# One core, fp32 layer step: the weights' sums of six block products made in the attention stage, the seven products in another order, the gated features' sums one stage later

## The reference, cut to what matters

```
xn = rms_norm(x, norm_mix_w)
rq, rk, rv, rg, cq, ckv, kpe, ga, gb = split_columns(xn @ w_in)
...
ret_y, mla_y, new_state = mixer_core(rq, rk, rv, q, ckv, kpe, w_ukv)
ret_branch = (head_group_norm(ret_y, ret_gn_w).astype(x.dtype) * jax.nn.silu(rg)) @ w_ret_o
mla_branch = mla_y @ w_mla_o
merged = jax.nn.sigmoid(ga) * ret_branch + jax.nn.sigmoid(gb) * mla_branch
h = x + merged @ w_out
g, u = jnp.split(rms_norm(h, norm_ffn_w) @ w_gate_up, 2, axis=-1)
h = h + (jax.nn.silu(g) * u) @ w_down
```

## Time and profile before

| | us |
|---|---|
| median of 3 runs | 2095.4 (2094.5 to 2097.5) |
| the profiled execution | 2096.48 |
| its span in the profile | 2094.6 |
| PE busy in it | 2002.0 (96%) |
| DVE busy | 1319.5 (63%) |
| ACT busy | 796.8 (38%) |
| POOL busy | 632.2 (30%) |

### The profile page before, as it was taken

One profiled execution on the slowest core, in us unless ns is written; L12 is line 12 of the kernel. 1 busy time (PEld: TensorE's weight loads), 2 busy tenths in 40 slices (PEclk: granted clock), 3 DMA queues, 4 the chain that ended last, 5 costly groups with the idle time before them and its releaser, 6 DMA issues.

```text
span 2094.6 us, 35179 instructions
## 1 busy us (share of the span) xinstructions
PE 2002.0 (96%) x14160; PEld 1933.2 (92%) x14160; DVE 1319.5 (63%) x2002; ACT 796.8 (38%) x1390; POOL 632.2 (30%) x488
## 2 busy tenths in 40 slices
PE   8989999999999989799999989999999999999997
PEld 8978888889988989699999979999999999999997
DVE  6567776765555558977867896655555555432257
ACT  5334444442332245365554325534444444310010
POOL 0110000001343445725223663544444444200000
PEclk9999999999999999899999989899999999999999
DMA  8301010151444466654755533122323232663412
GB/s 308 110 24 32 24 32 25 34 216 45 139 164 163 165 247 206 233 192 150 256 208 181 189 120 133 57 99 93 116 88 121 84 125 84 246 256 113 173 54 86
DMA packets 114241, 282.37 MB, mean 135 GB/s; under 512 B 13344, under 2 KB 30688, under 8 KB 106528
## 3 DMA queue, kind: packets, MB, share of 16 engines
q1 hardware_dynamic: 114080, 280.12, 38.2%
HBM read 191.85 MB, written 88.23 MB: 134 GB/s over the span
## 4 chain that ended last, share of the span: by engine, by line
PE 79%; DVE 12%; issue 3%; ACT 2%; DMA 2%; POOL 1%; SPq 0%; DVEq 0%; ACTq 0%; POOLq 0%
PE ps L1148 24%; PE ps L1149 23%; PE ps L1150 23%; DVE s_lo L2133 1%; PE ps L1249 1%; PE ps L1341 1%; PE ps L1243 1%; DVE t_lo L2133 1%; DVE tmp L2140 1%; DVE hg L2498 1%; DVE hg L2490 1%; DVE negmax L2362 1%; DVE hg L2502 1%; DMA xn_lo<-xn_spill 1%; PE ps L1404 1%
## 5 line engine op out<-in xcount | busy, mean ns | idle before, releaser
L1148 PE MATMUL ps<-s_hi,t_hi 128*128 128x272 f32 x1344 | 395.8, 295 | 30.8 <-DVE s_lo L2133 30.8
L1149 PE MATMUL ps<-s_hi,t_lo 128*128 128x272 f32 x1344 | 393.9, 293 | 0.0
L1150 PE MATMUL ps<-s_lo,t_hi 128*128 128x272 f32 x1344 | 392.7, 292 | 0.0
L1148 PE MATMUL ps<-sx_hi,t_hi 128*128 128x272 f32 x1232 | 357.1, 290 | 0.0
L1149 PE MATMUL ps<-sx_hi,t_lo 128*128 128x272 f32 x1232 | 356.9, 290 | 0.0
L1148 PEld LDWEIGHTS ps<-s_hi,t_hi 128*128 128x128 f32 x1344 | 260.0, 193 | 33.7 <-DVE s_lo L2133 24.4
L1149 PEld LDWEIGHTS ps<-s_hi,t_lo 128*128 128x128 f32 x1344 | 259.6, 193 | 0.0
L1150 PEld LDWEIGHTS ps<-s_lo,t_hi 128*128 128x128 f32 x1344 | 259.5, 193 | 0.0
L1150 PE MATMUL ps<-sx_lo,t_hi 128*128 128x272 f32 x880 | 255.3, 290 | 0.0
L1148 PEld LDWEIGHTS ps<-sx_hi,t_hi 128*128 128x128 f32 x1232 | 234.8, 191 | 0.3 <-DVE t_lo L2133 0.2
L1149 PEld LDWEIGHTS ps<-sx_hi,t_lo 128*128 128x128 f32 x1232 | 234.3, 190 | 0.0
(11 more groups left out here) (283 smaller groups left out, 5114.8 us busy)
## 6 DMA issues: line engine op xcount, KB each, us to landing
t_row<-in_weights SPq DMA_DIRECT2D x48, 512.0 KB, 5.7
y_spill<-hg_r SPq DMA_DIRECT2D x44, 544.0 KB, 3.4
yd<-y_spill SPq DMA_DIRECT2D x22, 1088.0 KB, 5.6
s_raw<-s_x SPq DMA_DIRECT2D x21, 1088.0 KB, 5.8
w_stage<-in_weights SPq DMA_DIRECT2D x35, 512.0 KB, 3.9
raw<-in_weights SPq DMA_DIRECT2D x22, 512.0 KB, 5.2
hg<-in_weights SPq DMA_DIRECT2D x22, 512.0 KB, 5.3
d_stage<-in_weights SPq DMA_DIRECT2D x24, 384.0 KB, 3.0
```

Of the source, the lines that this page charges most:

```text
L1148: nc.tensor.matmul(out, wh, xh, start=start, stop=False, skip_group_check=onto)
L1149: nc.tensor.matmul(out, wl, xh, start=False, stop=False, skip_group_check=onto)
L1150: return nc.tensor.matmul(out, wh, xl, start=False, stop=stop, skip_group_check=onto)
```

## The change

The change has five parts.

1. **Jobs.** The weights' sums T of all six octets are made during attention, in 48 jobs. A job is one half (two of four 128-columns) of the four weights' blocks of one octet and one p: SP loads 2 x 256 KB into `job_tile[job % 2]`, POOL does four operations of 128x256, each on the result of the one before (`job_sums`), and SP stores 512 KB to `t_sums` in device memory. `job_slots` puts them at six T steps of each head (four in the last): `job_store(job - 1)`, then `job_load(job)`. The second tile is where `x_inv` was, which is stored and loaded again. While the jobs run, weights' items 9 to I_RET + 3 use a single stage (the load of item n waits for the low part of item n - 1). The rotary sum of heads 1 to 7 goes from POOL to DVE.
2. **Octets' rows.** POOL makes no T sums in the octets. Each step's row is loaded: three from the weights, four from `t_sums`, 84 loads of half rows in pairs over three `t_rows` buffers, each of which waits for the low part three steps before.
3. **Order of the seven products.** C11 is ready after step 1, C12 after 4, C22 after 5, C21 after 6 (before: C21 after 3, C11 after 4, C22 after 5, C12 after 6). ACT makes 4 copies an octet instead of 12, and DVE 24 reads of banks instead of 16; in MIX_OUT the first product is added to three results by 12 more DVE operations.
4. **Gated features' sums.** POOL's 16 operations on the gated features are done in GATE_A's units 4 to 19 instead of in GATE_RET's last units and GATE_A's first, and SP stores them at units 14 and 22.
5. **MIX_OUT and pair 0.** The merged features are no longer stored to `s_m` and loaded again, but are taken from SBUF; of the squares for the feed-forward norm 12 are made in MIX_OUT and 4 in pair 0; pair 0 takes its products in the order 0, 1, 3, 2, 5, 4, 6, with its fourth sums on DVE and its third on POOL.

```diff
-FIRST_ORDER = (0, 3, 2, 1, 4, 5, 6)
+FIRST_ORDER = (0, 1, 3, 2, 5, 4, 6)
...
-ROW_OF_STEP = (0, 0, 4, 4, 2, 1, 3)
-OPENING_STEPS = (0, 4, 5)
...
+OPENING_STEPS = (0, 2, 5)
+ROWS = 3
...
+SUM_PLACE = {2: 0, 6: 1, 3: 2, 5: 3}
+JOBS = OCTETS * 4 * 2
...
+RESULT_STEP = (1, 4, 5, 6)
+RESULT_OF = {1: C11, 4: C12, 5: C22, 6: C21}
...
+def job_slots():
+    steps = [(h, at) for h in range(MH) for at in ((0, 1, 3, 4, 6, 7) if h + 1 < MH else (0, 1, 3, 5))]
+    return {step: 2 + i for i, step in enumerate(steps)}
...
+FIRST_JOB_ITEM, LAST_JOB_ITEM = 9, I_RET + 3
...
+def stage_of(n):
+    return 0 if FIRST_JOB_ITEM <= n <= LAST_JOB_ITEM else n % 2
...
+        x_inv_spill = nc.dram_tensor("x_inv_spill", (P, TOK), F32, kind="Internal").ap()
+        t_sums = nc.dram_tensor("t_sums", (OCTETS, 4, P, 4, 4 * P), F32, kind="Internal").ap()
...
-                    sp.wait_ge(w_low, n - 1)
+                    sp.wait_ge(w_low, n if FIRST_JOB_ITEM <= n <= LAST_JOB_ITEM else n - 1)
...
-                if g == 0 and what == "M" and kind in "KR":
+                if what == "M" and (kind, g) == ("K", 0):
                     items(mla_item(h, kind) + 2, mla_item(h, kind) + 3)
+                if what == "M" and (kind, g) == ("V", NG - 1) and h % 2 == 0:
+                    items(mla_item(h, "R") + 2, mla_item(h, "R") + 3)
...
+            def job_store(job):
+                sp.wait_ge(job_sum, 4 * job + 4)
+                o, p, half = job // 8, job // 2 % 4, job % 2
+                sp.dma_start(t_sums[o, p, :, :, 2 * P * half:2 * P * (half + 1)], job_tile[job % 2][:, :, :])\
+                  .then_inc(job_out[job % 2], 16)
...
+            def job_load(job):
+                if job == 0:
+                    sp.wait_ge(w_low, FIRST_JOB_ITEM - 1)
+                elif job == 1:
+                    sp.wait_ge(spill_out, 16 * (2 * KT + 1))
+                else:
+                    sp.wait_ge(job_out[job % 2], 16 * (job // 2))
+                o, p, half = job // 8, job // 2 % 4, job % 2
+                first, step = OCTET_ITEMS[o]
+                first += step * p
+                for tile in range(2):
+                    sp.dma_start(job_tile[job % 2][:, 2 * tile:2 * tile + 2, :].rearrange("p h (k c) -> p h k c", c=P),
+                                 W[first + 4 * step * tile].rearrange("p (h k) c -> p h k c", h=2)
+                                 [:, :, 2 * half:2 * half + 2, :]).then_inc(job_in[job % 2], 16)
...
+                    if s[0] == "T":
+                        if (h, transposed) in slots:
+                            job = slots[h, transposed]
+                            job_store(job - 1)
+                            job_load(job)
+                        transposed += 1
...
-            def row_load(o, r, half):
+            def row_load(j, half):
...
+                if j >= ROWS:
+                    sp.wait_ge(ot_low, 4 * (j - ROWS) + 2 * half + 2)
...
+                if s in SUM_PLACE:
+                    src = t_sums[o, 2 * half:2 * half + 2, :, SUM_PLACE[s], :].rearrange("n p c -> p n c")
...
+                    if p in (0, 2) and j + ROWS < STEPS * OCTETS:
+                        row_load(j + ROWS, p // 2)
...
-            def quadrant_copy(o, c, p):
-                u = UNITS * o + 4 * (C11, C12, C22).index(c) + p
...
+            def first_product_copy(o, p):
+                u = UNITS * o + p
...
+                    if h:
+                        dve.wait_ge(p_free, own[u] + 1)
+                        dve.wait_ge(rot_low, r)
+                        nc.vector.tensor_tensor(rot_total[:, 0:c1 - c0], rot_cos[:, 0:c1 - c0], rot_sin[:, 0:c1 - c0],
+                                                ALU.add).then_inc(rot_sum, 1)
...
-            def result_read(o, c, p):
-                u = UNITS * o + 12 + 4 * c + p
...
+            def bank_read(o, s, p):
+                dve.wait_ge(oct_done, UNITS * o + 4 * s + p + 1)
                 bank = ps[:, 2 * p:2 * p + 2, 0:QUARTER]
+                c = {1: C11, 2: C21, 3: C22, 4: C12, 5: C22, 6: C21}[s]
+                if o == MIX_OUT:
+                    at = quarters(piece(o, c, p)[:, :])
+                    if s == 1:
+                        wait_piece(dve, o, c, p)
+                    nc.vector.tensor_tensor(at, bank, at, ALU.add).then_inc(o_read, 1)
...
+            def first_product_added(p):
+                dve.wait_ge(oct_done, UNITS * MIX_OUT + p + 1)
+                for c in (C12, C22, C21):
+                    wait_piece(dve, MIX_OUT, c, p)
+                    at = quarters(piece(MIX_OUT, c, p)[:, :])
+                    ins = nc.vector.tensor_tensor(at, ps[:, 2 * p:2 * p + 2, 0:QUARTER], at, ALU.add)
...
+            def job_sums(job):
+                b11, b21, b12, b22 = [job_tile[job % 2][:, i, :] for i in range(4)]
+                pool.wait_ge(job_in[job % 2], 32 * (job // 2 + 1))
+                nc.gpsimd.tensor_tensor(b22, b22, b12, ALU.subtract).then_inc(job_sum, 1)
+                pool.wait_ge(job_sum, 4 * job + 1)
+                nc.gpsimd.tensor_tensor(b12, b12, b11, ALU.subtract).then_inc(job_sum, 1)
+                pool.wait_ge(job_sum, 4 * job + 2)
+                nc.gpsimd.tensor_tensor(b11, b22, b11, ALU.add).then_inc(job_sum, 1)
+                pool.wait_ge(job_sum, 4 * job + 3)
+                nc.gpsimd.tensor_tensor(b21, b21, b11, ALU.subtract).then_inc(job_sum, 1)
...
-            def octet_sums(o, name, p):
-                b11, b12, b21, b22, t3 = [t_rows[r][:, p, :] for r in range(5)]
-                if name == "T3":
...
-                    nc.gpsimd.tensor_tensor(t3, b22, b12, ALU.subtract).then_inc(ot_sum, 1)
...
+            def gated_sums(name, p):
+                if name == "S1":
+                    wait_final(pool, GATE_RET, C21, p)
+                    nc.gpsimd.tensor_tensor(bm(C21, p), bm(C21, p), bm(C22, p), ALU.add).then_inc(m_sum, 1)
+                elif name == "S2":
...
+                    if o == GATE_A and 4 <= n < 20:
+                        gated_sums(("S1", "S2", "S3", "S4")[n % 4], n // 4 - 1)
```

More of the change, by code:

```diff
@@ new lines, in octet_transfers, with result_store @@
+                late, m = divmod(g - 5, UNITS)
+                if late == GATE_RET and m // 4 in (1, 4, 5) and m % 2:
+                    operand_store({1: 0, 4: 1, 5: 6}[m // 4], m % 4 // 2)
+                if o == GATE_A and n in (14, 22):
+                    for s in (2, 3, 4, 5):
+                        operand_store(s, n // 16)
+            def result_store(o, c, half):
+                tile, (c0, c1) = tile_of(c, 2 * half), tail_of(c)
+                sp.wait_ge(c_act, 16 * o + 4 * c + 2 * half + 2)
+                sp.dma_start(gate_spill[o - GATE_A, tile:tile + 2, :, c0:c1].rearrange("n p c -> p n c"),
+                             acc_tiles(c, slice(2 * half, 2 * half + 2))).then_inc(c_out[c], 16)
@@ L2067, in _ @@
                     act.wait_ge(y_done, 2 * pair)
[L2068 removed]
+                    part(u3, pair, "X")
                 if pair == 0:
@@ new lines, in bank_read @@
+                if s < 4 and o == GATE_A:
+                    wait_final(dve, GATE_RET, c, p)
+                elif s < 4 and o == GATE_B or (o, s) == (BRANCH_MLA, 1):
+                    dve.wait_ge(c_out[c], 32 if o == GATE_B else 64)
+                elif s in (2, 3) and o == BRANCH_RET:
+                    dve.wait_ge(c_out[c], 64)
+                elif s in (2, 3) and o == BRANCH_MLA:
+                    dve.wait_ge(m_gated, 4 * (c - 1) + p + 1)
+                if s > 1:
+                    kept = acc(C12, p) if s < 5 else acc(c, p)
+                    nc.vector.tensor_tensor(quarters(acc(c, p)), bank, quarters(kept), ALU.add).then_inc(o_read, 1)
+                elif o in (GATE_RET, GATE_A, GATE_B):
+                    if o == GATE_RET and p == 0:
+                        dve.wait_ge(consts_in, 64)
+                    nc.vector.tensor_tensor(quarters(acc(c, p)), bank, quarters(x_inv[:, 0:HALF]), ALU.mult)\
+                      .then_inc(o_read, 1)
+                else:
+                    wait_piece(dve, o, c, p)
+                    if o == BRANCH_RET and p == 0:
+                        for step in range(STEPS):
+                            dve.wait_ge(sm_out[step], SY_OUT)
+                    dst = bm(c, p) if o == BRANCH_RET else acc(c, p)
+                    nc.vector.tensor_tensor(quarters(dst), bank, quarters(piece(o, c, p)[:, :]), ALU.mult).then_inc(o_read, 1)
@@ L2573, in gated_low @@
+            for tiles in (slice(0, 2), slice(2, 4)):
+                operand_low(2, S2_AT - 2 + tiles.stop // 2, acc_tiles(C11, tiles), tiles)
+            for p in range(4):
+                fourth_sum(p)
             def gated_low(pair, half):
```

818 lines of the change are left out of this document (371 added, 447 removed).

## The result

| | us |
|---|---|
| kernel before, median of 4 runs | 2095.3 |
| changed kernel, median of 4 runs | 2138.1 (2137.0 to 2139.2) |
| ratio, with its 95% interval | 1.0201 (1.0188 to 1.0213) |
| span of its profile | 2135.3 |

The change makes the kernel slower by 2%, 42.8 us. The forecast was slower by 10.6 us with a range that ended at 2134, 4 us short. The profile's spans give the split: the first octet's first product starts at 839.1 us instead of 765.9, which is 73.2 us lost, and from there to the end it takes 1296.2 us instead of 1328.7, which is 32.5 won.

The account below looks back on a forecast made before the run. PE was taken to bound the kernel, its stalls being what can be won. From the profiled 2096.5 us, -31 for the octets and +42 for attention gave 2107.5, or 2106 against the median; range 2068 to 2134.

Parts of the forecast that it names:

- the octets' sum: GATE_RET to pair 0: PE's stalls and clock losses shrink, -31 us in sum, between -18 and -40.
- attention's term: Attention: the jobs' serial cycle delays the `xn_lo` loads and with them the kernel, +42 us.
- C: Attention: time of one job's cycle, L plus POOL's sums plus wakes; taken as 8.4 us, bounds 7.3 and 9.7.
- the hole beside `xn_hi`: End of attention: 5.6 us added to 41 cycles, about 4 for standing behind the jobs' and `xn_hi`'s bytes.
- behind `xn_lo`: After the `xn_lo` loads, up to the octets: no further delay was added.
- Rival 2: Octets: they bring 10 us instead of 31, the stall moving to DVE's added bank reads; 2127 us, chance 0.11.
- L: Job cycle: time from the store's issue to the second load's landing, taken as 5.1 us, bounds 4.0 and 6.3.
- rival 3: Attention: DVE slows POOL's four sums, adding 1.4 us to C, 58 us; above 2150; chance 0.06 with others.
- every microsecond of theirs is one of the kernel's: End of attention: PE already waits for the `xn_lo` loads, so their delay adds in full to the kernel's time.
- Rival 1: Attention: the jobs keep pace, C at 7.3 to 7.75, time some 2067 to 2079 us; chance 0.23.
- The prediction's own sign of being wrong: C at 7.6 or less, PE waiting more for DVE's negmax or `p_exp`, or stalls in GATE_B.
- The page's estimate: Job cycle: 2.0 us a transfer plus bytes at 436 GB/s gives L 4.4, C 7.7, total near 2077 us.

Follow-up runs that it names:

- run 4: Kernel before, with POOL's T sums in the octets cut to one column except four in GATE_RET: 2077.1 us, ratio 0.9916.
- run 5: Changed kernel without the 48 jobs, plus 30 POOL operations on idle scratch in GATE_RET and GATE_A: 2079.6 us, 12.7 more than without them.
- Run 9: Changed kernel in its own store-then-load order, with jobs seven to a head in heads 0 to 5 and four in head 6: 2156.6 us, ratio 1.0291.
- Run 10: The fastest version with the four POOL operations of each job cut to one column, all transfers kept: 2066.4 us.
- the fastest version: Changed kernel with each job's loads ahead of the previous job's store, seven jobs a head and four in head 6: 2077.5 us, ratio 0.9916.

## Why the prediction was wrong

The mechanism, the sign and the octets' sum were right; the size of attention's term was not: forecast +42, measured +73.2, and this error of 31 us put the time outside the range. By place it is 16.7 us from C, 5.3 from the hole beside `xn_hi`, 11.2 behind `xn_lo`, and 1.8 less at the start.

**The octets**, forecast -31: measured -32.5. By place: GATE_RET and GATE_A -5.8 and -16.7 (forecast -21 together), BRANCH_MLA and MIX_OUT -9.0 and +0.6 (forecast -8), pair 0 -1.2 (forecast -2), the rest of the feed-forward stages nothing. The stall in BRANCH_MLA went wholly, and what I left as stalls is all in MIX_OUT. That POOL beside DVE makes this stall was shown from both sides, by runs 4 and 5. Run 4 gives 20 of the 32 us to the T sums alone; most of GATE_RET's and BRANCH_MLA's came only with the order and the later gated sums. Rival 2, which left 21 us of the stall in place, is out.

**The cycle**, forecast C = 8.4 as L 5.1 + 0.1 + 3.2 + 0.05. (These make 8.45; taking 8.4 left out 2 us over 41 cycles.) Measured over the 40 cycles from the store of job 1 (137.90 us) to that of job 41 (490.64): 8.82 on average, which is 5.35 + 0.07 + 3.37 + 0.03. The row taken for L, a pair of 1088 KB, was near: in thirty of the forty cycles L is 5.0 to 5.4, 5.15 on average. In the other ten it is 5.56 to 6.95, and these lift its mean to 5.35. What they share is open: three of them have nothing on SP between the loads and the next store. And where DVE works beside POOL, a sum takes up to 1.2 us instead of 0.74 (the one at 146.77 us takes 1.22, with DVE's `w_lo` at 146.69 to 147.38). That is rival 3 in small, 0.17 us to a cycle instead of 1.4. Together 0.42 us times 40, 16.7 us: the step that failed is "I take 8.4", taken from one row where a mean over disturbed ones was needed, times 41.

**The hole beside `xn_hi`**: the 5.6 us that I added to 41 even cycles, 4 of them for standing behind bytes, are 7.8 in the 41st cycle (16.2 us) and 3.1 behind it. With these 5.3 us more, 16.7 from the mean of C and 1.8 less at the start, `xn_lo` came at 510.0 instead of the forecast 489.7.

**Behind `xn_lo`**: forecast nothing. Measured 11.2 us: the delay is 62.0 us at the issue of `xn_lo` and 73.2 at the octets' start. This second step failed too: "every microsecond of theirs is one of the kernel's" ended the sum at `xn_lo`. The late rows themselves add nothing: PE goes on behind them at 527.04 instead of 468.75, 58.3 us late (the last of them takes 11.6 us in the chain instead of 14.4). But the jobs 43 to 47 are not done, and their sums stand in POOL's program too, ahead of the retention's rotary sums (L2803). POOL, DVE and PE there:

```profile
551.08 0.99 POOL L2803 TENSOR_TENSOR rq<-tmp,tmp 128x384 f32<-128x384 f32 x1
552.18 0.56 DVE L2201 TENSOR_TENSOR tmp<-ps,cos 128x384 f32<-128x384 f32 x1 [13.44 <-POOL rq L2803]
553.97 0.55 PE L1203 MATMUL ps<-pt_hi,v_hi 128*128 128x256 f32 x1 [10.48 <-issue]
```

DVE had the products for L2803 ready at 534.9 us. POOL first summed two more jobs, waiting for their loads each time, and came to L2803 at 551.08. DVE stood for 13.4 us, and PE for 10.5, until DVE had read the bank at 553.9. The profile names nothing for PE's wait; in the program PE's unit there waits for the bank read of the unit before it, which is DVE's. The other 4.4 of the 14.9 us between 58.3 and 73.2 are open. Run 9, which has all jobs ahead of `xn_lo`, has no such wait and loses 2.4 us there instead of 11.2.

**Hidden under it**: DVE's contention with the jobs, which I put at some 3 us in attention once the jobs kept pace. Run 10 gives up to 11 us for it. Rival 1 was true of the design and not of the code: with the two calls swapped and the jobs at other places they keep pace, and the time of 2077.5 is in the 2067 to 2079 that I gave for this. That is luck in part: it comes from 11 us of POOL's sums and up to 4 of the other edits, and not from a cycle between 7.3 and 7.75. The prediction's own sign of being wrong, that PE waits for `p_exp` more than now, came as well, 24.4 us instead of 6.7; but 17.4 of them are the one wait behind `ym_spill` shown above.

**The page's estimate**, C = 7.7 by "DMA: Bandwidth & Descriptors" (section "Anatomy of one DMA") of the Trainium skill, which is given for transfers issued by GpSimd, was lower still. The trace of these, issued by SP, disagrees: L is 5.35 us on average and 5.0 at the least for 1 MB, against its 4.4. A part of this is that the second load of a job is issued only 1.3 us after the store, which its sum for one transfer doesn't have.

**The range** held too little of the high side. The bound of 9.7 for C was worked out, and the range's end corresponded to C of 9.1 with nothing behind `xn_lo`.

## What to carry to other kernels

Where idle engines are given background work in jobs, look at the issuing queue's program first: load ahead of the store that waits, or two buffers are worth one; here this one swap is worth 46 us. A cycle's price is multiplied by its count, so take it as a mean with the disturbances in it, and follow the delay to the last job, in every program in which jobs stand (POOL's here, beside SP's), not to the first late transfer. Work that is moved away from an engine's neighbour is paid for where it lands: the T sums cost some 18 us beside DVE in the octets (run 4), and up to 11 in attention (run 10).

## What the runs showed of the hardware

The issue of a job's load takes SP 0.83 us, that of its store 0.57, where the weights' items of twice a load's size take 0.43 and, in the kernel before, the `xn_lo` rows 0.45 each. The job's transfers are cut in runs of 1 KB (382 packets to 0.39 MB), the items in 4 KB by the program; that this is the reason was not tested. A POOL operation of 0.74 us took 1.22 beside DVE's `w_lo`, so that the two engines slow each other both ways. And three times the traffic in attention (0.53 instead of 0.17 of the DMA engines' time from 137 us on, in the fastest version) cost nothing that a run could tell, by run 10.
